# Expert weight blocks queued between the output blocks, with one buffer more, in a one-core hybrid layer

## The reference, cut to what matters

```python
# first block
h = h + mixer(rms_norm(h), w_in, ...)          # ends in einsum(mixed [256, 2048], w_out [2048, 1024])
h = h + expert_choice_ffn(rms_norm(h), w_router, w_gate, w_up, w_down)
# expert_choice_ffn: each of 16 experts takes its 32 best tokens
a = einsum('becd,edf->becf', xs, w_gate); u = einsum('becd,edf->becf', xs, w_up)      # d 1024, f 512
y = einsum('becf,efd->becd', silu(a) * u, w_down) * vals
# second block: for l in range(2): projections w_in_2[l], three attentions, gates, w_out_2[l]
```

## The kernel before, in words

| block | slot before | waits for | slot after | waits for |
|---|---|---|---|---|
| E0, E1 | 2, 3 | `mix_ssd`, behind O3 | 2, 3 | last state-space products, ahead of O2 |
| E2 | 0 | O3 read | 4 | `wo_read` 4, behind O2 |
| E3 | 4 | `out_pe` 4 | 5 (bias) | nothing |
| E4 | 1 | O2 read | 6 (strips) | `mixT_pe` 8, behind O3 |
| E5 | 5 (bias) | nothing | 1 | O2 read |
| E6 | 2 | E0 read | 0 | O3 read |
| E7 | 3 | E1 read | 2 | E0 read |
| E8 | 0 | E2 read | 3 | E1 read |
| E9 | 4 | E3 read | 4 | E2 read |
| E10 | 1 | E4 read | 1 | E5 read |
| E11 | 2 | E6 read | 0 | E6 read |
| W0 | 0 | E43 read | 0 | E46 read |
| W2 | 2 | E46 read | 2 | E47 read |

## Time and profile before

### The profile page before, as it was taken

The page is one execution under the profiler, slowest core; times in us unless marked ns, Lnnn a source line. Parts: engine busy times, 40 slices in busy tenths (PEclk is TensorE's granted clock), DMA queues, the critical chain, the costliest instruction groups (busy, mean ns, idle before and its releaser), DMA issues.

```text
span 1324.7 us, 18186 instructions
## 1 busy us (share of the span) xinstructions
PE 1207.5 (91%) x7510; PEld 926.0 (70%) x7510; DVE 671.2 (51%) x1087; ACT 420.9 (32%) x1002; POOL 334.7 (25%) x326
## 2 busy tenths in 40 slices
PE   6999799899989599978989999999988999999987
PEld 5888665677767332212229798999878989999877
DVE  2776857233495300001027255676787345567775
ACT  5447342233643410100014521311523451330432
POOL 0665730412310300000022113233253013314241
PEclk9999999999899799999998999999999999999999
DMA  6443244667306899999991525344332245435310
GB/s 203 137 150 134 89 123 173 213 230 272 135 18 237 317 406 421 422 421 422 421 407 53 212 68 195 128 145 174 128 116 88 80 160 183 146 122 191 128 64 33
DMA packets 91555, 257.03 MB, mean 194 GB/s; under 512 B 7645, under 2 KB 12534, under 8 KB 79058
## 3 DMA queue, kind: packets, MB, share of 16 engines
q1 hardware_dynamic: 89122, 248.67, 50.1%
q0 software_dynamic: 2032, 6.95, 1.6%
q10 hardware_dynamic: 320, 0.26, 0.1%
HBM read 253.49 MB, written 2.12 MB: 193 GB/s over the span
## 4 chain that ended last, share of the span: by engine, by line
PE 65%; DMA 14%; DVE 9%; ACT 5%; POOL 3%; issue 2%; SPq 1%; DVEq 0%; ACTq 0%; POOLq 0%
PE bank L705 61%; DMA ring<-in_w_up_dram 7%; PE bank L714 4%; DVE ring_r L2068 3%; DMA ring<-in_w_down_dram 3%; DMA ring<-in_w_ada_dram 2%; POOL late L2715 2%; POOL acc L2716 2%; DMA ring<-in_w_gate_dram 1%; ACT ring L1565 1%; DMA ring<-in_w_in_dram 1%; ACT L1565 1%; ACT oa L1565 1%; ACT qkT L1565 1%; DVE ring_r L2307 0%
## 5 line engine op out<-in xcount | busy, mean ns | idle before, releaser
L2824 POOL CAST w_hi_r<-ring 128x1024 fp32r<-128x1024 f32 x136 | 150.1, 1133 | 638.8 <-DMA ring<-in_w_in_dram 267.9
L705 PE MATMUL bank<-ring_r,xT_hi 128*128 128x256 f32 (+1 forms) x864 | 243.0, 281 | 0.0
L2068 DVE TENSOR_TENSOR ring_r<-ring,w_hi_r 128x1024 fp32r<-128x1024 f32 x136 | 186.3, 1399 | 52.1 <-POOL w_hi_r L2824 52.1
L705 PE MATMUL bank<-w_hi_r,xT_hi 128*128 128x256 f32 x704 | 205.1, 291 | 5.0 <-DVE xT_r L2073 1.9
L705 PE MATMUL bank<-w_hi_r,xT_r 128*128 128x256 f32 x704 | 199.7, 284 | 0.0
L705 PEld LDWEIGHTS bank<-ring_r,xT_hi 128*128 128x128 f32 x864 | 165.0, 191 | 0.2
L705 PEld LDWEIGHTS bank<-w_hi_r,xT_hi 128*128 128x128 f32 x704 | 134.1, 190 | 17.2 <-issue 9.3
L705 PEld LDWEIGHTS bank<-w_hi_r,xT_r 128*128 128x128 f32 x704 | 133.8, 190 | 0.0
L705 PE MATMUL bank<-ring,xsT 128*32 128x512 f32 x496 | 111.8, 594 | 19.4 <-DMA ring<-in_w_gate_dram 9.2
L705 PE MATMUL bank<-xT,ring 128*128 128x256 f32 x576 | 125.3, 379 | 0.3 <-DMA ring<-in_w_in_dram 0.3
L705 PEld LDWEIGHTS bank<-xT,ring 128*128 128x128 f32 x576 | 109.2, 190 | 15.1 <-DMA ring<-in_w_in_dram 0.4
(11 more groups left out here) (371 smaller groups left out, 2185.5 us busy)
## 6 DMA issues: line engine op xcount, KB each, us to landing
ring<-in_w_in_dram SPq DMA_DIRECT2D x39, 2048.0 KB, 8.0
ring<-in_w_up_dram SPq DMA_DIRECT2D x32, 1024.0 KB, 16.3
ring<-in_w_down_dram SPq DMA_DIRECT2D x32, 1024.0 KB, 16.9
ring<-in_w_gate_dram SPq DMA_DIRECT2D x30, 1024.0 KB, 16.6
ring<-in_w_ada_dram SPq DMA_DIRECT2D x12, 2048.0 KB, 9.3
ring<-in_w_out_dram SPq DMA_DIRECT2D x8, 2048.0 KB, 7.8
ring<-in_w_o_mla_dram SPq DMA_DIRECT2D x2, 2048.0 KB, 13.3
ring<-in_w_o_swa_dram SPq DMA_DIRECT2D x2, 2048.0 KB, 7.8
```

The lines of the kernel that those rows point to most:

```text
L705: return release(nc.tensor.matmul(o, lhsT, rhs, start=start, stop=stop))
L2068: tt(lo, raw_, hi.bitcast(F32), ALU.subtract).then_inc(lo_done.sem, lo_done.one("piece"))
L2824: nc.gpsimd.tensor_copy(hi, raw_).then_inc(hi_done.sem, hi_done.one("piece"))
```

## The change

Seven edits belong together:

- The slot of a block comes from `slot_of`: the first seven expert blocks take ring 2, 3, 4, bias, strips, ring 1, ring 0, and then the ring goes round as 2, 3, 4, 1, 0. The memory of `strips` is a slot of its own (6), used once, by E4.
- SP issues in the order of a list `issue`: O0, O1, **E0, E1**, O2, **E2, E3**, O3, **E4**, and then on in the plan's order.
- E0 no longer waits for the mixed product (`mix_ssd`) but for the last readers of rings 2 and 3 (`ssd_y_pe` 8 and `ssdy_dve` 4).
- E4, over `strips`, waits for the last transposes of the mixer's gates (`mixT_pe` 8), whose memory it shares.
- The first block in ring 4 waits for `wo_read` 4, no more for `out_pe` 4.
- To allow that, the rounded pieces q 4 to 15 stand in `wo_later`, in the dead part of `cT_r`; so `out_high` 4 to 7 wait for no earlier piece.
- POOL's load of the strips now also waits until PE has read E4.

```diff
+    opening, order = (2, 3, 4, RING, RING + 1, 1, 0), (2, 3, 4, 1, 0)
+
+    def slot_of(n):
+
+        if n < n1:
+            return n % 2
+        if n >= n2:
+            return (n - n2) % (RING - 1)
+        j = n - n1
+        return opening[j] if j < len(opening) else order[(j - len(opening)) % len(order)]
+
+    slot = [slot_of(n) for n in range(len(plan))]
+    over_strips = slot.index(RING + 1)
...
-        wo_home = [hq_r[:, i // 2, i % 2 * HI // 2:(i % 2 + 1) * HI // 2].rearrange("p (k n) -> p k n", k=2) for i in range(4)]
+            wo_first = [hq_r[:, i // 2, i % 2 * HI // 2:(i % 2 + 1) * HI // 2].rearrange("p (k n) -> p k n", k=2) for i in range(4)]
+            wo_later = [cT_r[:, VT0 + 4 * i:VT0 + 4 * i + 4, :].rearrange("p a n -> p (a n)").rearrange("p (k n) -> p k n", k=2)
+                        for i in range(4)]
...
+            ring += (strips[:].rearrange("p h n -> p (h n)"),)
...
-            for n, (name, _, _, nk, _, w) in enumerate(plan):
+            issue = list(range(n_out + 2)) + [n1, n1 + 1, n_out + 2, n1 + 2, n1 + 3, n_out + 3] + list(range(n1 + 4, len(plan)))
+            for n in issue:
+                name, _, _, nk, _, w = plan[n]
                 if slot[n] in slot[:n]:
                     sp.wait_ge(*block_free(max(m for m in range(n) if slot[m] == slot[n])))
                 if n == n1:
-                    sp.wait_ge(mix_ssd.sem, 1)
+                    sp.wait_ge(ssd_y_pe.sem, 8)
+                    sp.wait_ge(ssdy_dve.sem, 4)
+                if n == over_strips:
+                    sp.wait_ge(mixT_pe.sem, 8)
                 if n >= n1 and slot[n] == RING - 1 and RING - 1 not in slot[n1:n]:
-                    sp.wait_ge(out_pe.sem, 4)
+                    sp.wait_ge(wo_read, 4)
...
             def out_high(q):
 
                 act.wait_ge(landed[slot[n_out + q // 4]], arrived(n_out + q // 4))
-                act.wait_ge(wo_read, q - 3)
+                if q >= 8:
+                    act.wait_ge(wo_read, q - 3)
...
             pool.dma_start(scratch[0:HS + HD, :], table[0:HS + HD, :]).then_inc(table_out, 16)
             pool.wait_ge(table_out, 16)
+            pool.wait_ge(*block_free(over_strips))
             pool.dma_start(strips[:], bass.AP(tensor=scratch.tensor, offset=0, ap=[[1, P], [2 * T, HS + HD], [1, BIAS_W]])
```

More of the change, by code:

```diff
@@ L186, in hybrid_kernel @@
     n1, n2 = (next(n for n, block in enumerate(plan) if block[0] == name) for name in ("w_gate", "w_in_2"))
-    slot = [n % 2 if n < n1 else RING if n == n1 + 5 else (n - n1 + (2 if n < n1 + 5 else 1)) % RING if n < n2 else (n - n2) % (RING - 1) for n in range(len(plan))]
-    slot = [{4: 0, 0: 4}.get(s, s) if n1 <= n < n2 else s for n, s in enumerate(slot)]
+    opening, order = (2, 3, 4, RING, RING + 1, 1, 0), (2, 3, 4, 1, 0)
[8 more added lines that the diff above has]
+    over_strips = slot.index(RING + 1)
     ctx = ExitStack()
@@ L386, in hybrid_kernel @@
         load_x, load_eye, load_tri, load_rows, load_small = map(sem, ("load_x", "load_eye", "load_tri", "load_rows", "load_small"))
-        landed = [sem(f"landed{i}") for i in range(RING + 1)]
+        landed = [sem(f"landed{i}") for i in range(RING + 2)]
         used = sem("used")
@@ L500, in hybrid_kernel @@
         out_bank = [bank[i] for i in (5, 3, 6, 7)]
-        wo_first, wo_hi, wo_lo, wo_read = Steps(sem("wo_first"), "piece"), Steps(sem("wo_hi"), "piece"), Steps(sem("wo_lo"), "piece"), sem("wo_read")
+        wo_begin, wo_hi, wo_lo, wo_read = Steps(sem("wo_begin"), "piece"), Steps(sem("wo_hi"), "piece"), Steps(sem("wo_lo"), "piece"), sem("wo_read")
         n_out = next(n for n, block in enumerate(plan) if block[0] == "w_out")
@@ L506, in wo_piece @@
             n, at = n_out + q // 4, q % 4 * HI // 2
-            return [v[slot[n]][:, at:at + HI // 2].rearrange("p (k n) -> p k n", k=2) for v in (ring, ring_r)] + [wo_home[q % 4]]
+            return [v[slot[n]][:, at:at + HI // 2].rearrange("p (k n) -> p k n", k=2) for v in (ring, ring_r)] + [(wo_later if q >= 4 else wo_first)[q % 4]]
         out_pe = Steps(sem("out_pe"), "q")
@@ L2305, in out_low @@
                 raw_, lo, hi = wo_piece(q)
-                dve.wait_ge(*((wo_first.sem, q + 1) if q < 4 else (wo_hi.sem, q - 3)))
+                dve.wait_ge(*((wo_begin.sem, q + 1) if q < 4 else (wo_hi.sem, q - 3)))
                 tt(lo, raw_, hi.bitcast(F32), ALU.subtract).then_inc(wo_lo.sem, wo_lo.one("piece"))
@@ L2783, in _ @@
                 raw_, _, hi = wo_piece(q)
-                nc.gpsimd.tensor_copy(hi, raw_).then_inc(wo_first.sem, wo_first.one("piece"))
+                nc.gpsimd.tensor_copy(hi, raw_).then_inc(wo_begin.sem, wo_begin.one("piece"))
             pool.wait_ge(out_dve.sem, 4)
```

## The result

| | before | changed |
|---|---|---|
| median of 7 runs, us | 1329.92 | 1335.26 |
| lowest to highest, us | 1327.87 to 1332.28 | 1333.36 to 1339.75 |
| profiled execution, us (span) | 1326.47 (1324.7) | 1334.13 (1332.3) |

The ratio is 1.0053, 95% interval 1.0036 to 1.0070. Twelve more runs of the same kernel gave 1.0047 (1.0028 to 1.0066). The change costs 0.5%, some 6 to 7 us by these ratios, where a median of 1328.5 us (1325.4 to 1332.9) was predicted, nothing gained or lost. The base moved too: the prediction started from a median of 1328.63 over three runs of the kernel before, and over seven it is 1329.92, so 1.3 of the 6.8 us between 1328.5 and 1335.3 are not the change's.

A forecast was written before the change was run, and what follows sets the result against it. The weight stream was taken to bound the kernel, 4.97 us a block. Without the strips 2.8 us gained, 2.7 us stay for them: 0.1 us earlier, so the median 1328.63 becomes 1328.5 us, range 1325.4 to 1332.9.

The forecast's parts named there:

- A: Stretch from O3's issue to PE's first matmul on the experts; forecast 0.9 us longer.
- B: Stretch from PE's first expert matmul to the first matmul behind E47; forecast 1.0 us shorter.
- C: Stretch from the first matmul behind E47 to the first attention matmul; forecast unchanged.
- E10: Expert weight block whose refill was forecast issued at 488.1 and landed at 496.0 without the strips, against 498.8 before.
- E47: Last expert weight block, which the attention layers follow; forecast to land at 682.5 against 682.6, 0.1 us earlier.
- What it costs the output projection: O3 behind two expert blocks lands 1.5 us later, 0.6 covered; projection, router and PE's expert start shift 0.9 us.
- rival three: O2 shares the DMA engines with the two expert blocks behind it; 7 us lost, 1335.6 us; chance 0.07 with unnamed mishaps.
- The refills: Later expert blocks are issued on PE's reads of before plus 0.9 us; without the strips the gain would be 2.8 us.
- E7: Expert weight block refilled once PE has read the first one; forecast issued at 464.4, landed at 472.3.
- The strips: POOL's load, released at 484.7 after the fifth expert block's read: 3.9 us fall in the gap, 2.7 stay in the stream.
- Rival two: The strips' first bytes come over 5.1 us after issue (2.4 reckoned), over 2.7 us slower, up to 1333.0; chance 0.13.
- The end: W0 waits for a later expert block; its first rounding is ready at 691.3, DVE wants it at 693.19: costs nothing.

The follow-up runs named there:

- one_head: The changed kernel with the strips load cut to one head of twelve, the other eleven set to zero on POOL; ratio to before 1.0019.
- the two repairs alone: The changed kernel with O3 issued ahead of the two expert blocks before it, and W0 in an earlier-released slot; ratio to before 1.0013.
- before_again: The kernel before run once more with no edit; ratio to before 1.0009.
- w0_rot: The changed kernel with the slots of attention blocks W0 to W3 dealt in another order, W0 in an earlier-released one; ratio to before 1.0034.

## Why the prediction was wrong

The sum was -0.1 us; the stretches give +4.9: A +1.9, B +1.5, C +1.6, where the forecast had +0.9, -1.0 and 0. None of it is a rival that was named. Three terms were mis-sized, by 1.0, 2.5 and 1.6 us, all in the same direction: the landing of O3, the landing of E10 and with it of E47, and the lateness of W0, which was put at nothing.

- **What bounds the kernel** was right: the weights from 476 (in the changed kernel from 497) to E47, three matmuls and a transfer at a time, 37 blocks in 184.3 us behind E10 (forecast 183.8). Early issue in itself was worth nothing, as said.
- **What it costs the output projection** (forecast 0.9 for A). O2 kept its 7.7 us and rival three fell. O3 was to land 9.2 us after its issue; it took 9.4 to 10.6, 9.9 on average. Against the profiles with O3 ahead of the expert blocks that is 2.2 us more. By its sixteen parts, 1.0 of them is the first part coming later (8.1 to 8.5 us after the issue, not 7.2 to 7.5), and 1.2 are the last part coming further behind the first (1.3 to 2.2 us, not 0.3 to 0.7). The forecast added bytes to lone landings and had no term for the second. The cover was there, somewhat less than reckoned (0.4 instead of 0.6): in the changed profile O3 lands 1.7 us later behind its issue than before, and the router's first transposes come 1.3 us later behind it.
- **The refills** (B). The releases were right to a few tenths. E0 starts at 465.69, 5.5 us behind the 460.2 of the forecast (4.8 for O3's later issue and 0.7 more in A); with those, E7 was due at 469.9 and went at 469.91, E10 due at 493.6 and went at 493.82. The step that failed is "landed at 496.0", with the strips 498.7, on the shifted clock 504.2; E10 landed at 506.4, **2.2 us** later, and to E47 another 0.5 came. The strips were not it: their 2.7 us in the stream measured as 2.1 to 2.4 (the 6.6 us behind the 2.7 came by subtraction, 2.36 MB at 421 GB/s are 5.6), and in one_head, almost without them, E10 took 9.5 us where 7.9 and some 0.5 for the one head were due. The landing was put together from lone transfers (7.9 us, parts within 0.3 to 0.8 us of each other) and then set against 498.8 of before, counted back from E47 in a full stream, where the parts are 2.5 us apart and the last one counts. The two are on different footings: in the changed profile the parts of E10's first half are 0.6 us apart, those of its second half 1.9 and those of E47's last transfer 2.4, and this growth of 1.8 us was taken for a gain. What the other 0.9 us are the runs don't separate.
- **The page's figure for a lone block.** The Trainium skill, page "DMA: Bandwidth & Descriptors", section "Anatomy of one DMA — SWDGE (gpsimd) path", gives its 2.0 us and 436 GB/s for transfers that GpSimd issues. The blocks are issued by SP, so the 6.8 us of the prediction are the page's for another path, and the 7.7 and 8.0 us don't speak against it.
- **The strips** were released when forecast (484.7 + 5.5 = 490.2; 490.93), and their first bytes came 1.8 us later (reckoned 2.4). Rival two, a late start, was not it.
- **The end** (forecast nothing for C). W0 was issued at 690.5 and landed at 698.3, as "682.1 ... 690.1" says with 8.1 us added. "DVE wants it at 693.19, 1.9 us cover it: nothing" looked at the first piece alone. POOL rounds eight pieces in a row, the row shows the first four of them, and where they end is what counts: 10 us later than before, beside the split that PE waits for.
- **The range.** Its upper end took the bounds of two terms (a shift of 1.5, all of the strips in the stream), 1332.9. The landing of O3 had no bound over 1.5, that of E10 none but the strips' bytes, and W0 none at all, so 1335.3 lay outside. The chance of slower, 0.20, was too small for a change whose gains and losses nearly cancelled while three of its terms could only go up.

## What to carry to other kernels

A landing reckoned from a lone transfer can't be set against one counted back in a full stream: take both from the same regime, or add the spread of the parts. Where a block is given the slot of a later release, follow every instruction that hangs on it, to where the last piece is done and what runs beside it, not the first piece alone. And dead memory used as one more buffer is worth what its rightful load can still do in time: with the first block in it instead of the fifth the stretches came out 4.4 us shorter than with the two repairs alone (288.9 against 293.3).

## What the runs showed of the hardware

- **TensorE's first matmuls run at one of two rates, and when it changes is chance.** In these profiles the 32 small ones take 3.8 to 7.1 us, whatever the kernel, and from the first of them to `tri` it is 24.4 to 29.7 us. Where the trace has a record of the granted clock there, it agrees: in before_again 0.50, the 1.2 GHz level, from 18.5 to 25.3 us, and 1.00, the 2.4 GHz level, behind it. The column reads 1.00 also ahead of a trace's first record, whatever the rate; in the changed profile the first one, of 1.00, starts at 26.8 us, in that of before at 16.6 (four us from 16.00, before and changed; 29 against 16 matmuls started):

```profile
16.00:20.00 4.00, 3.18 (x29) 3.18 (x29) 0.00 (x0) 2.27 (x4) 0.00 (x0) 1.00 1.06 411
```

```profile
16.00:20.00 4.00, 3.45 (x16) 3.45 (x17) 0.00 (x0) 1.99 (x4) 0.00 (x0) 1.00 1.06 410
```

  so the column can't show it there, the durations do: about 0.11 and 0.21 us a matmul, a factor of two as between the two levels. PE had done 16 transposes and then stood for 0.9 us in both. The Trainium skill, page "TensorE: Matmul & The Clock Gate", Part 1, says that the array starts at 1.2 GHz and that the point of the change depends on where the first matmul falls in a window that runs free of the kernel's start; that the point moves from profile to profile agrees. The same part puts this at half a microsecond either way; here the rise lies 10.2 us apart in the profiles of before and changed, and the measurement decides.
- **The sixteen parts of a transfer drift apart in a full stream and stay so**: 1.6 to 2.5 us from about 511 on and 2.0 to 2.7 at E47, against 0.3 to 1.0 for one that finds the DMA engines idle. A step of 0.6 to 1.8 us comes at a 16 KB transfer of the instruction queue in ten of twelve profiles.
- **POOL's roundings beside DVE** take 1.49 us instead of 1.00 (5.97 and 3.99 for four, changed kernel and w0_rot), DVE's cast beside them 0.91 instead of 0.43.
